# The three merge products as seven half-size products each, and eight modulation columns computed in the down projection

## What is computed

```python
def merge_branches(y_rnn, y_na, g_rnn, g_na, w_rnn_out, w_na_out, w_out):
    merged = jax.nn.sigmoid(g_rnn) * (y_rnn @ w_rnn_out) + jax.nn.sigmoid(g_na) * (y_na @ w_na_out)
    return merged @ w_out
...
        x = x + mx[2] * merge_branches(y_rnn_x, y_na_x, mrx, mnx, w_rnn_out[l], w_na_out[l], w_out[l])
        x = x + mx[5] * conv_ffn(modulate(x, norm_ffn_g[l], mx[3], mx[4]), w_up[l], ffn_conv_w[l], ffn_conv_b[l], w_down[l])
```

## Time and profile before

| | |
|---|---|
| median of three runs | 2133.1 us |
| the profiled execution | 2134.98 us, span 2133.2 us |
| PE busy | 96% of the span |
| DVE, ACT, POOL busy | 77%, 50%, 23% |
| granted PE clock, mean | 0.994 |
| mean DMA rate | 113 GB/s |

### The profile page before, as it was taken

One profiled execution on the slowest core, in us unless ns is written; L12 is line 12 of the kernel. 1 busy time (PEld: TensorE's weight loads), 2 busy tenths in 40 slices (PEclk: granted clock), 3 DMA queues, 4 the chain that ended last, 5 costly groups with the idle time before them and its releaser, 6 DMA issues.

```text
span 2133.2 us, 28319 instructions
## 1 busy us (share of the span) xinstructions
PE 2054.4 (96%) x10618; PEld 1740.1 (82%) x10618; DVE 1632.6 (77%) x2809; ACT 1072.4 (50%) x1631; POOL 495.6 (23%) x377
## 2 busy tenths in 40 slices
PE   5899999999999999999998899999999999999999
PEld 1778888988988889888887788887788888887887
DVE  6688598596785985958858866667998888877876
ACT  3466566665766666656666621002544334434332
POOL 0031130222112302222123010000124442115650
PEclk9999999999999999999999999999999999999999
DMA  8421211112012120120111285454347764239663
GB/s 327 112 56 48 62 41 46 57 52 70 30 41 64 48 61 32 53 70 30 43 50 63 93 321 196 148 177 141 89 134 191 181 177 122 94 118 340 221 206 128
DMA packets 105576, 241.65 MB, mean 113 GB/s; under 512 B 27264, under 2 KB 32768, under 8 KB 104960
## 3 DMA queue, kind: packets, MB, share of 16 engines
q1 hardware_dynamic: 74304, 191.08, 26.5%
q0 software_dynamic: 14592, 44.05, 7.9%
q10 hardware_dynamic: 16544, 4.72, 1.0%
HBM read 203.11 MB, written 63.96 MB: 125 GB/s over the span
## 4 chain that ended last, share of the span: by engine, by line
PE 77%; DVE 12%; ACT 4%; issue 2%; DMA 1%; POOL 0%; SPq 0%; ACTq 0%; DVEq 0%; POOLq 0%
PE banks L47 14%; PE banks L48 14%; PE banks L49 14%; PE banks L991 4%; PE banks L862 4%; PE banks L864 4%; PE banks L863 4%; PE banks L895 3%; PE banks L2269 3%; PE banks L2270 3%; PE banks L2271 3%; DVE probT_low L1493 2%; PE banks L953 2%; DVE prob L1485 1%; PE banks L935 1%
## 5 line engine op out<-in xcount | busy, mean ns | idle before, releaser
L47 PE MATMUL banks<-qh,xnh 128*128 128x384 f32 (+1 forms) x640 | 223.0, 348 | 0.3 <-PEq L216 0.3
L862 PE MATMUL banks<-xnh,wh 128*128 128x512 f32 (+1 forms) x536 | 211.9, 395 | 4.4 <-ACT stage L1097 4.1
L49 PE MATMUL banks<-qh,xnl 128*128 128x384 f32 (+1 forms) x640 | 207.4, 324 | 0.0
L48 PE MATMUL banks<-ql,xnh 128*128 128x384 f32 (+1 forms) x640 | 207.3, 324 | 0.0
L864 PE MATMUL banks<-xnh,wl 128*128 128x512 f32 (+1 forms) x536 | 204.8, 382 | 0.0
L863 PE MATMUL banks<-xnl,wh 128*128 128x512 f32 (+1 forms) x536 | 204.4, 381 | 0.0
L1493 DVE TENSOR_TENSOR probT_low<-banks,probT_high 128x512 fp32r<-128x512 f32 (+2 forms) x256 | 138.8, 583 | 56.2 <-ACT probT_high L1165 55.2
L1165 ACT CAST probT_high<-banks 128x512 fp32r<-128x512 f32 (+2 forms) x256 | 117.0, 510 | 59.9 <-PE banks L953 50.9
L47 PE MATMUL banks<-yh,wh 128*128 128x512 f32 x372 | 144.9, 389 | 0.9 <-DVE wl L2471 0.9
L48 PE MATMUL banks<-yl,wh 128*128 128x512 f32 x372 | 144.8, 389 | 0.0
L49 PE MATMUL banks<-yh,wl 128*128 128x512 f32 x372 | 144.8, 389 | 0.0
(11 more groups left out here) (396 smaller groups left out, 6021.9 us busy)
## 6 DMA issues: line engine op xcount, KB each, us to landing
raw<-w_ff SPq DMA_DIRECT2D x33, 512.0 KB, 5.2
down_d<-w_down POOLq DMA_DIRECT2D x66, 256.0 KB, 6.7
raw<-w_fm SPq DMA_DIRECT2D x32, 512.0 KB, 6.6
extras<-h_d SPq DMA_DIRECT2D x55, 256.0 KB, 4.0
raw<-w_qkv SPq DMA_DIRECT2D x24, 512.0 KB, 3.9
raw<-w_mix SPq DMA_DIRECT2D x24, 512.0 KB, 4.8
h_d<-conv_d SPq DMA_DIRECT2D x21, 512.0 KB, 3.1
raw<-w_modT SPq DMA_DIRECT2D x16, 512.0 KB, 4.8
```

What stands on the lines that cost most here:

```text
L47: pe.matmul(out, w_hi(k), x_hi(k), start=(k == 0), stop=False)
L48: pe.matmul(out, w_hi(k), x_lo(k), start=False, stop=False)
L49: last = pe.matmul(out, w_lo(k), x_hi(k), start=False, stop=(k == chunks - 1))
L862: pe.matmul(out, fh[:, s, k, :], xnh[:, k, c0:c1], start=(k == 0), stop=False)
```

## The change

Each of the three merge products becomes seven products of 512 x 512 x 512: LEFT, RIGHT, SUM_2, SUM_3, SUM_1, CORNER, SUM_4 (p is 0 to 6), four steps of 128 rows each, so 84 steps s for the three phases ph. A step makes 12 matmuls (`times`). Raw buffers form a ring of 8 (`STEP_RING`) and split operands one of 6 (`SLOTS`). What each engine does for it:

- SP loads for each step half a buffer of weights, straight from `w_mix` or from the sums in `mix_d`, and for LEFT, RIGHT and SUM_4 the tokens beside them; for the five mixed products of phases 0 and 1 it loads a block `extras` instead. In phase 2 the tokens come from the tile `merged`.
- POOL makes the token sums of the mixed products (`token_mix`, 60 of 128 x 512), multiplies the sums of products with the gates (`gate_block`, 16 of 128 x 1024), and adds squares and parts of the output at the end. In turns 1 to 6 of the mixer it issues the 96 transfers that make the weight sums.
- ACT splits all of a step's buffer (`split_high`), copies LEFT's product out of PSUM, scales parts and squares at the end.
- DVE splits all of a step's buffer (`split_low`), combines the seven products in pairs of PSUM banks (`combine`), adds the two gated branches (`merge_add`), and makes 24 of the modulation columns. The last eight (those of `mx[5]`) are made at steps 16 to 23 of the down projection, whose SP program loads their rows.
- In the mixer's last turn four steps are split in place of eight token blocks and two weight blocks. PE multiplies one output block of LEFT there in four pieces, and a second one ahead of the last `weighted_values`.

```diff
+            def left_piece(m, k):
+
+                hi, lo = early_slot(k)
+                out = every[:, 7 if m == 3 else m, :]
+                if m == 3 and k == 0:
                     pe.wait_ge(f_free, f_count(PAIRS - 1, LAST_MN + 1))
-                pe.wait_ge(y_lo, k + 1)
-                pe.matmul(F_ps, fh[:, 0, k, :], yh[:, k, 0:HALF], start=(k == 0), stop=False)
-                pe.matmul(F_ps, fh[:, 0, k, :], yl[:, k, 0:HALF], start=False, stop=False)
-                done = pe.matmul(F_ps, fl[:, 0, k, :], yh[:, k, 0:HALF], start=False, stop=(k == KC - 1))
-                if k == KC - 1:
-                    done.then_inc(mix_full, 1)
+                elif k == 0:
+                    pe.wait_ge(bound_done, PAIRS * ATT)
+                pe.wait_ge(step_lo, k + 1)
+                moving = lambda a: a.rearrange("p k c -> p (k c)")[:, HALF:T]
+                pe.matmul(out, hi[:, m, :], moving(hi), start=(k == 0), stop=False)
+                pe.matmul(out, hi[:, m, :], moving(lo), start=False, stop=False)
+                done = pe.matmul(out, lo[:, m, :], moving(hi), start=False, stop=(k == KC // 2 - 1))
+                if k == KC // 2 - 1:
+                    done.then_inc(mix_product, 1)
...
+            def step_high(s):
+                act.wait_ge(step_in[s], 32)
+                act.wait_ge(f_full, full_count(PAIRS - 1, (LAST_MR if s == 0 else LAST_MN) + 1))
+                act.copy(early_slot(s)[0].rearrange("p k c -> p (k c)"), step_raw_of(s)).then_inc(step_hi, 1)
...
-                    elif u % 2 == 1:
-                        y_high(u // 2)
-                    elif u in (2, 6):
-                        mix_high(u // 4)
+                    elif u in (3, 5, 7, 9):
+                        step_high((u - 3) // 2)
...
+        def slot_released(engine, s):
+            d = s - SLOTS
+            if d < 0:
+                engine.wait_ge(y_done, mixer_done)
+            elif d % 4 == 3:
+                engine.wait_ge(full, 4 * (d // 4 + 1))
+            else:
+                engine.wait_ge(step_used, d + 1 - (d + 1) // 4)
+
...
+            def load_step(s):
+                g, ph, p, k = of(s)
+                if s >= STEP_RING:
+                    sp.wait_ge(step_lo, s - STEP_RING + 1)
+                    _, ph0, p0, _ = of(s - STEP_RING)
+                    if p0 == LEFT and ph0 < 2:
+                        sp.wait_ge(mixed, mix_count(s - STEP_RING))
+                if s == 2 * 4:
+                    sp.wait_ge(mix_sums, 16 * 8 * 3 * KC // 2)
+                if s == MIX_STEPS:
+                    sp.wait_ge(yn_out[0], PAIRS * 32)
+                    sp.wait_ge(yn_out[1], PAIRS * 32)
+                a, b = KC * ph + k, KC * ph + KC // 2 + k
+                weights_at = (w_mix[a, :, low], w_mix[b, :, low], mix_d[ph, 1, k], mix_d[ph, 2, k], mix_d[ph, 0, k],
+                              w_mix[b, :, high], mix_d[ph, 3, k])[p]
+                to = step_raw_of(s % STEP_RING)
+                sp.dma_start(to[:, low], weights_at).then_inc(step_in[s % STEP_RING], 16)
...
+                if p in DIRECT:
+                    chunk, cols = {LEFT: (k, low), RIGHT: (4 + k, low), SUM_4: (4 + k, high)}[p]
+                    if ph == 2:
+                        sp.wait_ge(merged, {LEFT: 1, RIGHT: 5, SUM_4: 3}[p] + k // 2)
+                        tokens_at = mg[:, chunk, cols]
+                    else:
+                        tokens_at = (yr_d, yn_d)[ph][chunk, :, cols]
...
+            sp.wait_ge(yr_out, PAIRS * 16)
+            load_step(4)
+            load_extra(0)
+            sp.wait_ge(y_done, mixer_done)
+            sp.wait_ge(stage_out, PAIRS * 64)
+            sp.wait_ge(yn_out[0], PAIRS * 32)
+            sp.wait_ge(yn_out[1], PAIRS * 32)
+            load_step(5)
+            load_extra(1)
+            sp.dma_start(sc[:, :], bass.AP(tensor=c_rows.tensor, offset=0, ap=[[0, P], [1, D]])).then_inc(c_in, 16)
+            load_row(0)
+            load_step(6)
+            load_extra(2)
+            load_row(1)
+            load_step(7)
+            load_extra(3)
+            for e in range(AUX_RING):
+                load_aux(sp, e)
+            load_extra(4)
+            for s in range(STEP_RING, MIX_LAST):
+                load_step(s)
...
+                elif p == SUM_2:
+                    pool.wait_ge(mixed, mix_count(s - 8))
+                    pool.tensor_tensor(mix, mix, other, ALU.subtract).then_inc(mixed, 1)
+                else:
+                    pool.wait_ge(mixed, 20 * ph + 4 + k + 1)
+                    pool.wait_ge(step_lo, s - STEP_RING + 1)
+                    pool.tensor_tensor(part, mix, other, ALU.add).then_inc(mixed, 1)
...
+            def gate_block(e):
+                ph, i = divmod(e, 8)
+                pool.wait_ge(combined, combined_count(7 * ph + BLOCK_PRODUCTS[i // 2], i % 2))
+                pool.wait_ge(aux_in[e % AUX_RING], 32 + e // AUX_RING * 16 + 16)
+                part = row_pair(mg, i) if ph == 0 else blocks[:, i % 2, :, :]
+                pool.tensor_tensor(part, part, aux[:, e % AUX_RING, :, :], ALU.mult).then_inc(gated, 1)
...
+        def times(pe, s, m):
+            g, k = divmod(s, 4)
+            hi, lo = slot(s)
+            out = bank(g, m)
+            if k == 0:
+                bank_free(pe, g, m)
+            pe.matmul(out, hi[:, m, :], line(hi)[:, high], start=(k == 0), stop=False)
+            pe.matmul(out, hi[:, m, :], line(lo)[:, high], start=False, stop=False)
+            last = pe.matmul(out, lo[:, m, :], line(hi)[:, high], start=False, stop=(k == 3))
+            if k == 3:
+                last.then_inc(full, 1)
+            elif m == (2 if g == 0 else 3):
+                last.then_inc(step_used, 1)
...
+                if s == 82:
+                    scale_part(0)
+                    scale_part(1)
+                    square(act, 8)
+                    scale_part(2)
+                    scale_part(3)
+                    square(act, 9)
+                split_high(s)
...
+            def split_low(s):
+                _, ph, p, k = of(s)
+                hi, lo = (line(a) for a in slot(s))
+                dve.wait_ge(step_hi, s + 1)
+                dve.wait_ge(step_in[s % STEP_RING], step_raw(s))
+                if p in MIXED and p != LEFT:
+                    dve.wait_ge(mixed, mix_count(s))
+                if p == SUM_2:
+                    dve.tensor_tensor(lo[:, low], step_raw_of(s % STEP_RING)[:, low], hi[:, low].bitcast(F32), ALU.subtract)
+                    dve.tensor_tensor(lo[:, high], mixes[:, k, :], hi[:, high].bitcast(F32), ALU.subtract)\
+                       .then_inc(step_lo, 1)
+                else:
+                    dve.tensor_tensor(lo, step_raw_of(s % STEP_RING), hi.bitcast(F32), ALU.subtract).then_inc(step_lo, 1)
...
+                if p == RIGHT:
+                    dve.wait_ge(taken, 2 * ph + j + 1)
+                    dve.tensor_tensor(to, u, b, ALU.add).then_inc(combined, 1)
+                else:
+                    dve.wait_ge(combined, combined_count(g - 1, j))
+                    if p == SUM_2:
+                        dve.tensor_tensor(u, u, b, ALU.add).then_inc(combined, 1)
+                    elif p == SUM_3:
+                        dve.tensor_tensor(v, u, b, ALU.subtract).then_inc(combined, 1)
+                    elif p == SUM_1:
+                        dve.tensor_tensor(to, b, v, ALU.subtract)
...
+            for s in range(4, MIX_LAST):
+                if s == 82:
+                    for m in range(3):
+                        corner_last(dve, m)
+                split_low(s)
+                g, r = divmod(s - 8, 4)
+                if g >= 0 and r in (1, 2) and g != 18:
+                    combine(g, r - 1)
+                    if g == 15:
+                        gated_left(r - 1)
+                    elif g == 17:
+                        gated_corner(r - 1)
+                if s == 81:
+                    combine(18, 0)
+                    combine(18, 1)
+                for i in add_at.get(s, ()):
+                    merge_add(i)
+                if s in columns_at:
+                    column(columns_at[s])
+                    if columns_at[s] == KC - 1:
+                        dve.wait_ge(mod_done, KC)
+                        dve.tensor_scalar(minus[:, :], mod[:, 2 * KC:3 * KC, 0], -1.0, None, ALU.mult).then_inc(parted, 1)
...
+                if s < STEP_RING + KC:
+                    n = s - STEP_RING
+                    sp.dma_start(gate_rows[:, n, :], w_modT[3 * KC + n]).then_inc(gate_in, 16)
...
+                if 16 <= s < 16 + KC:
+                    n = s - 16
+                    if n == 0:
+                        dve.wait_ge(gate_silu, GATE_SILU)
+                        dve.wait_ge(gate_in, GATE_IN)
+                    mod_column(dve, 5 * KC + n, n % 2, gate_rows[:, n, :], silu_row, gate_dots, bm, mod, gate_dotted,
+                               merge_mod, GATE_DONE + n + 1)
```

834 lines of the change are left out of this document (493 added, 341 removed).

## The result

The changed kernel takes 2206.0 us (median of 4 runs, 2204.39 to 2207.79), the kernel before 2133.8: a ratio of 1.0343, 95% interval 1.033 to 1.0356. It is slower, as forecast, but by 72 us and not by 26, and it lies outside the range (2125 to 2190). The profiled execution took 2207.79 us, with a span of 2206.0.

A forecast was written before the change was run, and what follows sets the result against it. PE bounds the old merge; in the new one DVE, excluding POOL on SBUF operands, sets the pace. 2134.98 + 27.7 (merge) - 5 (last turn) + 2 (norm) + 1.5 (down projection) = 2161.2 us, median 2159; range 2125 to 2190.

The forecast's parts named there:

- the signs that the prediction named: Merge: about 285 us, PE mainly waiting for DVE's split, DVE over 90% busy, longer splits and token sums, 9 us start wait.
- The middle: Merge steps 8 to 79: DVE's own 169.2 us plus 67 for being held by POOL, 236.2 us.
- The upper bound of 269: Merge steps 8 to 79: DVE's 169.2 us plus all 100 us of POOL's work, none hidden.
- The start: Merge, from the last `weighted_values` to step 8's split: 23.3 us, with 6.5 MB of transfers ahead; PE waits some 9.
- The forecast of P + 19 without the gate blocks: Merge start: step 8's split 19 us after the last `weighted_values` if gate blocks did not stand ahead, instead of 23.3.
- The end: Merge, step 79's split to the last matmul: 26 us in place of 19.8, as ACT's scalings delay step 82.
- The last turn: Mixer's last turn: fewer DVE splits, so -5 us (0 to -7).
- The 96 transfers of the weight sums: Mixer turns 1 to 6: POOL issues them under an existing wait, 0 us (to 3 if a gate value comes late).
- The norm: Norm: square sums move to POOL beside DVE's scalings, +2 us (0 to 6).
- The down projection: Down projection: eight added columns and 4.5 MB more transfers, +1.5 us (0 to 6).
- Rival 1: Merge: PE stays the bound, POOL mostly running where DVE waits or reads PSUM; 2110 us, chance 0.15.
- Rival 3: Merge phases 0 and 1: transfers set the pace, a price of 15 to 50 us, chance 0.05.

The follow-up runs named there:

- e2_pool: Changed kernel with GpSimd's merge token sums (but the first four) and gate multiplications computed over only 16 columns: 2152.3 us, ratio 1.0087.
- e6_dve_sums: Changed kernel with the merge's token sums and gate multiplications moved from GpSimd to VectorE, sums two steps ahead: 2178.0 us, ratio 1.0207.
- e9_ahead: Changed kernel with GpSimd making each token sum two steps earlier, ahead of gate multiplications: 2199.3 us, ratio 1.0314.
- e8_start: Changed kernel with ScalarE's LEFT copies at steps 5 and 6, step 8's extra block loaded earlier, three gate blocks behind step 13: 2199.8 us, ratio 1.0312.
- e11_orders: Changed kernel with the edits of e4_store, e8_start and e9_ahead, and VectorE's combines ahead of splits: 2196.1 us, ratio 1.0298.
- e4_store: Changed kernel with the first gate block's store issued ahead of four loads in the mixer's last turn: 2198.4 us, ratio 1.0312.
- e14_both: Changed kernel with e2_pool's cut, and the merge's 24 modulation columns computed over 16 of 1024 elements: 2146.8 us, ratio 1.0067.
- e5_warm: Changed kernel with 205 further matmuls added ahead of TensorE's waits in the merge: 2206.7 us, ratio 1.0344.

## Why the prediction was wrong

The side and the mechanism held: VectorE and GpSimd exclude each other on SBUF operands, VectorE sets the pace and the merge loses more than PE saves. e2_pool shows it by taking the one away, e6_dve_sums by moving it. Of the signs that the prediction named, splits over 1.22 us (1.51 in the largest group), combines that keep it (1.21) and token sums towards 2.2 (1.80 to 2.12) came. Three did not. PE's waits at the start are 21 us (2.9 and 18.1), not 9, the longer one behind ScalarE's copy; its other large waits are for combines, not for splits; and VectorE is busy for 82% of the merge (88% of its middle), not for over 90%. The last is the step that failed. Four terms were off.

- **The middle, +24.8 us, the step that failed most: VectorE's waits were put at nothing.** The sum was VectorE's own 169.2 plus 67 for being held, with VectorE busy throughout. Measured: its own work 173.9 (e2_pool), held 55 (229.1 - 173.9), and 32 us of waits that the sum did not contain. So the charge for GpSimd was not too small but 12 us too large; the waits alone outweigh the whole miss. By what released them, some 15 of the 32 us hang on GpSimd's sums, directly or through ScalarE's half: a sum (1.8 us, held up itself) must end before the split, and a gate multiplication (3.1 to 3.2 us) stands ahead of the next sum. Another 6.5 are for modulation rows from DMA, 5.1 for the first loads of `merged` in phase 2 (4.9 of these stand in e6_dve_sums too, where GpSimd has next to no work), and 3.5 stand behind a slot that PE had not yet freed. e9_ahead shows that 6 us of the waits can be had by order; the rest of this split was only read from the trace. The upper bound of 269 that the prediction named contains the measured 261, but it assumed no waits either.
- **The start, +5.7: the amount of the transfers.** The forecast was 6.5 MB at 365 GB/s; the trace has 8.1 MB at 357 (see e8_start). Its 26 blocks of 256 KB are 6.8 MB, not 6.5, and step 4 with its extra, 0.8 MB, was still in the queue at P + 3.6. What makes up the last 0.5 MB stays open. The forecast of P + 19 without the gate blocks was too early as well: with these and four loads of weights moved away the split begins at P + 23.0 and 23.5. Of these 5 to 6 us little reached the end: 3.4 in e8_start, and 2.2 of the merge in e11_orders, where the middle is 259.9 us and the end 33.6.
- **The end, +6.3.** ScalarE's eight scalings delayed step 82 as I had said (its split ends at 1525.44, 14.1 us after step 79's, forecast 16). But the split of step 83 took 3.39 us beside GpSimd's addition of a part (1524.31 to 1527.65), and the matmuls behind it shared their time with the norm's small ones, the first of them at a low clock. From the critical chain, and GpSimd's row:

```profile
1520.56 1.93 ACT held_products L2051 x3
...
1523.01 0.94 ACT late_operands L2035
...
1525.36 3.39 DVE late_operands L2115
...
1528.79 0.79 PE banks L1984
```

```profile
1524.31 3.34 POOL L1939 TENSOR_TENSOR x<-x,blocks_c 128x1024 f32<-128x1024 f32 x1
```

- **The last turn, +3.3 in place of -5.** I took VectorE's removed splits as a gain of 5; they brought 1.9 (e4_store against before). The other 5.2 are the store of the gate block, late behind four new loads; the prediction counted operations and matmuls for this turn and nothing of SyncE's queue. The 96 transfers of the weight sums cost nothing, as forecast: through the first seven turns the changed kernel keeps its distance to the one before within 0.07 us.

The norm is right (+2.3 for +2). The up projection is 414.0 to 414.1 us in all runs against 412.5 before, which I did not forecast and did not pursue. The down projection's +4.1 lies within its term's 0 to 6; its cause stays open.

Rival 1, 2110 us, was not to be had: it took 15 us for start and end, where e14_both, with PE as the bound, has some 36 (38 less 2 of waits in the middle), the lower clock included. Rival 3 was no cause in the middle, where transfers show at one place once POOL's work is gone; at the start they were what was mis-sized. The clock was in no term, and e5_warm says that this was right for the middle; in e14_both, where PE is the bound, its 13 us are likely real, which no run tested.

## What to carry to other kernels

Fewer matmuls are worth what the other engines can deliver: add up VectorE's operations with two SBUF operands (small ones and fused ones too) and GpSimd's as if they were one engine, and add waits where the two feed each other. If work must be given to one of them, VectorE's 0.7 us may be cheaper than GpSimd's 1.3 to 2.1 beside it. A stage that starts from data just stored and ends block by block pays its start and end again: here some 36 us, against a saving of 32.6. Of every load that is put ahead of a store in a queue, ask who waits for the store. And where an issuing engine waits, look whether the DMA engines were idle before you call that wait a cause.
